# Two blocks on one core: the second projection of the last feed forward by seven products instead of eight, its sums split between VectorE, ScalarE and transfers

## The reference

```python
        h = h + rmsnorm(m, post_mix_g[l])
        f = rmsnorm(h, pre_ff_g[l]) @ w_ff1[l]          # 1024 -> 4096
        f = jnp.square(jax.nn.relu(f)) @ w_ff2[l]       # 4096 -> 1024
        h = h + rmsnorm(f, post_ff_g[l])
```

## Time and profile before

| | us |
|---|---|
| median of 3 runs | 1729.57 (1729.56 to 1731.13) |
| the profiled execution | 1730.73 |
| its span in the profile | 1729.0 |
| TensorE busy | 1715.3 (99%) |
| VectorE busy | 1209.1 (70%) |
| ScalarE busy | 820.2 (47%) |
| GpSimd busy | 46.4 (3%) |
| moved by transfers | 181.36 MB, 105 GB/s in the mean |

### The profile page before, as it was taken

The page is one execution under the profiler, slowest core; times in us unless marked ns, Lnnn a source line. Parts: engine busy times, 40 slices in busy tenths (PEclk is TensorE's granted clock), DMA queues, the critical chain, the costliest instruction groups (busy, mean ns, idle before and its releaser), DMA issues.

```text
span 1729.0 us, 26320 instructions
## 1 busy us (share of the span) xinstructions
PE 1715.3 (99%) x10458; PEld 1497.2 (87%) x10458; DVE 1209.1 (70%) x1975; ACT 820.2 (47%) x1449; POOL 46.4 (3%) x103
## 2 busy tenths in 40 slices
PE   9999999999999999999999999999999999999998
PEld 8777788999999887777989999989888898999997
DVE  4588787777787735666877777868446876677776
ACT  4477744444445235664444444443565555333342
POOL 0212000000000000000000000000000000000000
PEclk9999999999999999999999999999999999999999
DMA  8343332333334232224133333352314224333331
GB/s 276 113 134 118 119 89 87 109 98 110 101 99 153 86 105 84 81 91 122 39 103 98 110 110 97 99 165 82 110 44 140 63 73 126 106 98 98 100 109 49
DMA packets 220125, 181.36 MB, mean 105 GB/s; under 512 B 9906, under 2 KB 178771, under 8 KB 220003
## 3 DMA queue, kind: packets, MB, share of 16 engines
q1 hardware_dynamic: 217954, 175.48, 33.1%
q0 software_dynamic: 2048, 4.20, 0.9%
HBM read 173.32 MB, written 7.38 MB: 105 GB/s over the span
## 4 chain that ended last, share of the span: by engine, by line
PE 93%; DVE 4%; ACT 1%; DMA 1%; issue 1%; POOL 0%; DVEq 0%; POOLq 0%
PE ps L733 29%; PE ps L734 28%; PE ps L735 28%; PE ps L1092 1%; PE ps L1137 1%; PE ps L1163 1%; PE ps L1112 1%; PE ps L1151 1%; DMA arena<-arena 1%; PE ps L987 1%; DVE wlo L1701 0%; DVE xl L1793 0%; PE ps L1102 0%; PE ps L972 0%; ACT whi L1321 0%
## 5 line engine op out<-in xcount | busy, mean ns | idle before, releaser
L1701 DVE TENSOR_TENSOR wlo<-raw,whi 128x1024 fp32r<-128x1024 f32 (+1 forms) x276 | 317.6, 1167 | 181.3 <-ACT whi L1321 181.0
L733 PE MATMUL ps<-xh,whi 128*128 128x256 f32 (+1 forms) x1016 | 332.4, 327 | 2.3 <-DVE xl L1793 2.3
L735 PE MATMUL ps<-xh,wlo 128*128 128x256 f32 (+1 forms) x1016 | 326.1, 321 | 0.0
L734 PE MATMUL ps<-xl,whi 128*128 128x256 f32 (+1 forms) x1016 | 325.9, 321 | 0.0
L1321 ACT ACTIVATE whi<-raw 128x1024 fp32r<-128x1024 f32 (+1 forms) x276 | 274.6, 1007 | 80.9 <-DMA raw<-in_w_ff 36.4
L733 PE MATMUL ps<-whi,hh 128*128 128x512 f32 x728 | 288.7, 397 | 1.4 <-DVE wlo L1701 1.3
L734 PE MATMUL ps<-wlo,hh 128*128 128x512 f32 x728 | 285.2, 392 | 0.0
L735 PE MATMUL ps<-whi,hl 128*128 128x512 f32 x728 | 283.6, 390 | 0.0
L733 PEld LDWEIGHTS ps<-xh,whi 128*128 128x128 f32 x1016 | 194.1, 191 | 25.8 <-issue 8.8
L735 PEld LDWEIGHTS ps<-xh,wlo 128*128 128x128 f32 x1016 | 194.1, 191 | 14.4
L734 PEld LDWEIGHTS ps<-xl,whi 128*128 128x128 f32 x1016 | 194.4, 191 | 12.2
(11 more groups left out here) (272 smaller groups left out, 2935.3 us busy)
## 6 DMA issues: line engine op xcount, KB each, us to landing
raw<-in_ffn_w_in SPq DMA_DIRECT2D x88, 512.0 KB, 3.8
raw<-in_w_ff SPq DMA_DIRECT2D x64, 512.0 KB, 4.2
raw<-in_ffn_w_out SPq DMA_DIRECT2D x44, 512.0 KB, 3.9
raw<-in_a_w_qkv SPq DMA_DIRECT2D x22, 512.0 KB, 5.5
raw<-in_w_in SPq DMA_DIRECT2D x20, 512.0 KB, 3.8
raw<-in_kv_w SPq DMA_DIRECT2D x16, 512.0 KB, 4.1
bias_skewed<-bias_rows SPq DMA_DIRECT2D x8, 640.0 KB
arena<-arena POOLq DMA_DIRECT2D x64, 64.0 KB, 2.7
```

Of the source, the lines that this page charges most:

```text
L733: e.matmul(o, ah, bh, start=start, stop=False, **more)
L734: e.matmul(o, ah, bl, start=False, stop=False, **more)
L735: return e.matmul(o, al, bh, start=False, stop=stop, **more)
L1701: e.tensor_tensor(lo[:, 0:n], src, f32(hi[:, 0:n]), ALU.subtract).then_inc(s.lo, 1)
```

## The change

In groups 1 to 6 the second projection is computed as products of 2 x 2 blocks: tokens 0 to 255 and 256 to 511 by block pairs (b, b+1) and (b+2, b+3) on the left, block pairs by output halves on the right. Seven products take the place of eight (`SEVEN`): a11, a12, s1, s4, s2, s3, a22, each 2 token tiles x 2 blocks x 3 matmuls. Groups 0 and 7 stay as they were.

- **Left sums** (s1, s2, s4, s3): VectorE, `left_sum`, from the unsplit hidden values. Every left operand then gets a high part (ScalarE) and a low part (VectorE) of its own (`left`), issued two products ahead. So the hidden blocks are not split any more when they are made, and `hidden_words` keeps them in float32.
- **Right sums**: B11 + B12, then + B22, then + B21 in one buffer, B12 + B22 in another. SP loads weight tiles into the four parts of `x`, POOL adds the others to them by transfers that add (`accum_op`). Every right operand is split as any weight.
- **Result sums**: two PSUM chains of two banks. After a11, a12 and a22 VectorE adds the bank to the left columns of `mb`. After s1, s4, s2, s3 ScalarE copies the bank with a sign to one of four buffers, and POOL adds this to the right columns of `mb` by a transfer. s4, s2, s3 and a22 go on in the bank that has just been read.
- **Relu and Square** of a pair's blocks move from VectorE to ScalarE (`square_hidden`), where they belong to these groups.
- `x` is written to DRAM ahead of the feed forward and read back at its end (`park`, `unpark`); the last gain vector is loaded late; `FEED_PIECES` becomes "2212", 14 pieces in a turn of two pairs.
- Weights lie in DRAM tile by tile, 4 KB in a row for each partition, so each load is one plain transfer. Some semaphores are shared, and the triangle of the mixer is loaded later.

```diff
-FEED_PIECES = ["1111"] + ["2222"] * 13
+FEED_PIECES = ["1111"] + ["2212"] * 13
+SEVEN_FIRST, SEVEN_LAST = 1, 6
+SEVEN = [("a11", 0, True, 0, 0, 1), ("a12", 1, True, 0, 0, 1), ("s1", 1, True, 1, 1, -1), ("s4", 1, False, 0, 1, -1),
+         ("s2", 0, False, 0, 1, -1), ("s3", 0, False, 1, 1, -1), ("a22", 0, False, 1, 0, 1)]
...
+        rights = [Right(a, ("load", landed), [(a, "a", (first, 1))]), Right(b, ("load", b_need), (), b_next),
+                  Right(a, ("a", 48 * turn + 16), [(a, "a", (last, 1))]),
+                  Right(c, ("load", c_need), [(d, "d", (last, 1))], c_next),
+                  Right(a, ("a", 48 * turn + 32), [(a, "a", (last, 0))]), Right(d, ("d", 16 * turn + 16), (), d_next),
+                  Right(a, ("a", 48 * turn + 48), (), following)]
...
+        for n, (name, chain, start, m, nh, sign) in enumerate(SEVEN):
+            u = 7 * (g - SEVEN_FIRST) + n
+            unit = self.unit("seven", rights[n], None)
...
+            for t in range(2):
...
+                self.step("seven", piece)
...
+                self.step("seven_post", piece)
+                self.flush()
+                if t == 1:
+                    self.left(u + 2)
+                yield
...
+            elif what == "seven":
...
+                w.wait_ge(s.lo, p.unit + 1)
+                w.wait_ge(s.left_lo, p.u + 1)
...
+                for k in (0, 1):
+                    m = mm3(e, ps[b][:], lh[:, k, c], ll[:, k, c], wh[:, k, :], wl[:, k, :], p.start and k == 0, k == 1,
+                            skip_group_check=True)
...
+            elif what == "left":
+                u, name, b, entry, (sem, value), free = arg
+                w.wait_ge(self.events[sem], value)
+                if free:
+                    w.wait_ge(s.rows, free)
+                e.activation(self.left_parts(entry)[0], self.left_source(name, b), ACT.Copy).then_inc(s.left_hi, 1)
...
+                e.activation(self.evict_to(p.sent), ps[p.bank][:], ACT.Copy, scale=float(p.sign)).then_inc(s.evicted, 1)
...
+            elif what == "square_hidden":
...
+                w.wait_ge(s.combined, pair.combined[3])
+                e.activation(first, first, ACT.Relu).then_inc(s.act, 1)
...
+                e.activation(second[:, 256:512], second[:, 256:512], ACT.Relu).then_inc(s.act, 1)
...
+                e.activation(self.hidden_words[:, pair.blocks[0], :], first, ACT.Square).then_inc(s.relu, 1)
...
+                e.activation(self.hidden_words[:, pair.blocks[1], :], second, ACT.Square).then_inc(s.relu, 1)
...
+                if name == "s1":
+                    e.tensor_tensor(tmp, a22, a21, ALU.subtract).then_inc(s.left_sum, 1)
+                elif name == "s2":
+                    e.scalar_tensor_tensor(tmp, tmp, -1.0, a11, ALU.mult, ALU.subtract).then_inc(s.left_sum, 1)
+                elif name == "s4":
+                    e.scalar_tensor_tensor(a12, a12, -1.0, tmp, ALU.mult, ALU.subtract).then_inc(s.left_sum, 1)
+                else:
+                    e.tensor_tensor(a21, a11, a21, ALU.subtract).then_inc(s.left_sum, 1)
...
+                e.tensor_tensor(self.mb[:, p.tile, 0:512], self.mb[:, p.tile, 0:512], ps[p.bank][:],
+                                ALU.add).then_inc(s.fadd, 1)
...
+                e.tensor_tensor(lo, self.left_source(name, b), f32(hi), ALU.subtract).then_inc(s.left_lo, 1)
...
+                    if chain == "a":
+                        w.wait_ge(s.lo, m + 1)
+                    else:
+                        w.wait_ge(s.right[buffer], right.before)
+                    e.dma_start(self.x[:, buffer, :], self.row_tile(*source),
+                                accum_op=ALU.add).then_inc(s.right_sum[chain], 16)
...
+                e.dma_start(self.mb[:, p.tile, p.nh * 512:p.nh * 512 + 512], self.evict_to(p.sent), accum_op=ALU.add).then_inc(s.added[p.sent % 4], 16)
...
+            e.dma_start(self.raw[:, m % RAW, :], ap["c_tiles"][m]).then_inc(s.raw[m % RAW], 16)
...
+            elif what == "park":
+                w.wait_ge(s.add, 8)
+                for t in range(4):
+                    e.dma_start(self.parked[t * 128:t * 128 + 128, :], self.x[:, t, :]).then_inc(s.x, 16)
```

More of the change, by code:

```diff
@@ L61, in __init__ @@
         self.kind, self.nh, self.t, self.bank, self.i = kind, nh, t, bank, i
-        self.norm, self.group, self.value = norm, group, None
+        self.norm, self.group, self.value, self.added = norm, group, None, None
+class Piece:
+    def __init__(self, u, unit, t, bank, start, before, value, tile, nh, sign, sent, earlier, after):
+        self.u, self.unit, self.t, self.bank, self.start, self.before, self.value = u, unit, t, bank, start, before, value
+        self.tile, self.nh, self.sign, self.sent, self.earlier, self.after = tile, nh, sign, sent, earlier, after
+class Right:
+    def __init__(self, buffer, need, sums=(), load=None):
+        self.buffer, self.need, self.sums, self.load, self.before = buffer, need, sums, load, None
 class Pair:
-    def __init__(self, kind, n, table, columns, blocks):
+    def __init__(self, kind, n, table, columns, blocks, first=None):
         self.kind, self.table, self.columns, self.blocks = kind, table, columns, blocks
@@ L350, in rows @@
                 self.step("rows_post", r)
+                if kind == "f" and group == 0:
+                    self.plain_rows = r.value
             yield
@@ L466, in attention_a, with seven, ring @@
         self.run(out)
+    def seven(self, g):
+        def ring(n):
+            k = SEVEN_FIRST + n // 3
+            return None if k > SEVEN_LAST else (n % 2 + 2, (4 * k + (2, 2, 0)[n % 3], (0, 1, 1)[n % 3]))
+        first, last = 4 * g, 4 * g + 2
+        turn, a = g - SEVEN_FIRST, g % 2
+        needs = []
+        for n in range(3):
+            r = 3 * (g - SEVEN_FIRST) + n
+            self.ring_need[r % 2] += 16
+            needs.append((r % 2 + 2, self.ring_need[r % 2], ring(r + 2)))
+        (b, b_need, b_next), (c, c_need, c_next), (d, d_need, d_next) = needs
+        following = (a, (4 * g + 8, 0)) if g + 2 <= SEVEN_LAST else None
+        landed = turn // 2 * 16 + 16
+        rights = [Right(a, ("load", landed), [(a, "a", (first, 1))]), Right(b, ("load", b_need), (), b_next),
[3 more added lines that the diff above has]
+                  Right(a, ("a", 48 * turn + 48), (), following)]
+        rights[3].before = d_need
+        if g == SEVEN_FIRST:
+            self.left(1)
+        for n, (name, chain, start, m, nh, sign) in enumerate(SEVEN):
+            u = 7 * (g - SEVEN_FIRST) + n
+            unit = self.unit("seven", rights[n], None)
+            if g == SEVEN_LAST and n == 6:
+                self.step("gain", self.fifth)
+                self.step("unpark", unit)
+            for t in range(2):
+                if (chain, t) not in self.chains:
+                    self.chains[chain, t] = self.bank(hold=True)
+                bank, tile = self.chains[chain, t], 2 * m + t
+                value, sent = self.count("rows") + 1, self.count("sent") if nh else None
+                after = ("evicted", sent + 1) if nh else ("fadd", self.count("fadd") + 1)
+                piece = Piece(u, unit, t, bank, start, self.evicts.get(bank), value, tile, nh, sign, sent,
+                              self.added.get((tile, nh)), after)
+                self.evicts[bank], self.added[tile, nh] = after, sent if nh else after[1]
+                self.step("seven", piece)
+                if t == 1:
+                    self.done(unit, "rows", value)
+                    self.entry_free[self.entry_of[u]] = value
+                if g == SEVEN_LAST and n == (3 if chain else 6):
+                    self.release(bank)
+                self.step("seven_post", piece)
+                self.flush()
+                if t == 1:
+                    self.left(u + 2)
+                yield
@@ L1314, in scalar @@
                     w.wait_ge(s.raw[tile % RAW], self.raw_at[tile])
+                elif kind == "seven":
+                    what, value = tile.need
+                    w.wait_ge(s.right[tile.buffer] if what == "load" else s.right_sum[what], value)
                 else:
@@ L2259, in sync @@
                 m, = arg
-                _, _, tile = self.plan.units[m]
+                kind, right, tile = self.plan.units[m]
+                if kind == "seven" and right.load is not None:
+                    w.wait_ge(s.hi, m + 1)
+                    w.wait_ge(s.lo, m + 1)
+                    rows_load(*right.load)
                 if tile is not None and tile + RAW < len(self.plan.tiles):
```

379 lines of the change are left out of this document (273 added, 106 removed).

## The result

Changed: 1754.11 us median of 4 runs (1750.48 to 1754.74), before: 1729.72 (1729.56 to 1731.13). The ratio is 1.0135, 95% interval [1.0117, 1.0152]. The change makes the kernel 24 us slower, where 13 were forecast. The profiled execution of the changed kernel took 1750.48 us, its span is 1748.8 with a mean granted clock of 0.996; the other three runs have 0.992 to 0.994, and no trace of them is kept.

What follows compares the result with a forecast made beforehand. TensorE's matmul stream was taken as the bound: 1730.7 - 16.3 (matmuls removed) + 19.0 (turns) + 3.0 (group 6) + 7.5 (clock) = 1743.9, median given as 1743 us. Forecast range 1733 to 1755, overall 1715 to 1763.

Steps and rivals of the forecast that it cites:

- The waits before s1: TensorE in each turn: about 1 us before s1 for a PSUM bank, the rest of 3.8 us before s3.
- the hole: VectorE idle 2.6 us after a pair's last addition, waiting for ScalarE's left high part behind Relu and Square.
- the turn: Two first-projection pairs plus one second-projection group, repeating: 42.08 us before, 39.36 without waits, about 44 to 45 forecast.
- A small wait of some 0.8 that I find before the next a12 is swallowed by the slower matmuls: In the turns, a wait of some 0.8 us before the next a12 was taken to cost nothing beside the slow clock.
- Group 1's first products start behind plain rows with room to spare: 0.: At the entry into the changed groups, no extra waiting of TensorE was expected: 0 us.
- Group 6, 3 us in bounds of 1 to 5: Last changed group: no weight sums for a further pair, but the bank wait and a closely following weight sum remain: +3 us.
- The clock, 7.5 in bounds of 0 to 10: Slower granted clock behind the waits before s3, 1.5 us in each of five turns: +7.5 us.
- If each brings the same: Each gap before s3 was assumed to lose 1.5 us of clock, like the earlier 1.83 us gap before this feed forward.
- granted clock near 0.9 in the stretch: Sign that would show the forecast right: granted clock near 0.9 over the changed stretch of the profile.
- Transfers: Adding 512 KB transfers for second weights: landing in about 5 us, wanted after 5.9, so no cost; 8.4 would hold ScalarE 2.5.
- transfers late: Rival: sums land in 8.4 us or transfer engines are full, 1758 us, with both 1763; range 1755 to 1765, chance 0.20.
- chain hidden, full gain: Rival: hand-overs between engines never hold TensorE, giving 1713 us; chance 0.22 for hidden wholly or in part.

Runs made afterwards that it cites:

- both orders: Changed kernel with the left part two products ahead split before the deferred Relu and Square, and left sums issued half a product earlier: 1730.41 us, ratio 0.9999.
- the square later too: On top of both orders, the deferred Relu and Square also stand behind the split of the next weights: 1726.63 us, ratio 0.9976.
- small transfers: Adding transfers cut to 8 columns, their number and waits kept: on the changed kernel 1748.31 us, on the square later too 1721.44 us.
- later splits: The square later too, two steps moved at group 1's start, group 6's second weights' splits one or two products later: 1720.71 us, ratio 0.9943.

## Why the prediction came out as it did

- **Direction and mechanism: right, by experiment.** TensorE bound, 16.3 us of matmuls out, and a chain of in-order hand-overs that gives back more. Orders alone, with the work the same, took back 24 us (both orders) and 28 (the square later too), 16.3 and 18.6 of them in idle time. The waits before s1 (0.92 with the restart, 1 forecast) and s3 (2.7, 2.8 forecast), the hole (2.57, 2.6 forecast) and the turn (44.8, 44 to 45 forecast) are in the trace.
- **"A small wait of some 0.8 that I find before the next a12 is swallowed by the slower matmuls": the step that failed in the turns.** It stands before a11, costs 0.66 to 1.05, and is swallowed by nothing, since by then the clock is back. 3.9 us. That the turn came out as forecast is therefore in part luck: this wait stands where more of the clock's loss was expected.
- **"Group 1's first products start behind plain rows with room to spare: 0."** Mis-sized: 4.5 us, of which the forecast had about 1 in the turns' 19. VectorE stood 4.7 us for the high part of a12's weight, which ScalarE had behind an eviction and the squares, and then had the sums, splits and additions at once. I had followed a turn in its steady state and not the entry into it.
- **Group 6, 3 us in bounds of 1 to 5:** 4.6, and 5.5 with the bank wait before s1 that the forecast had in this term, so above its upper bound. The reason was only half right: besides the bank and the sum, ScalarE's queue puts evictions behind waits for landings. The runs with small transfers and with later splits give 4 to 5 us for it, clock included.
- **The clock, 7.5 in bounds of 0 to 10:** 4.8 in the profiled run, some 9 in the median. "If each brings the same" was wrong: of five equal gaps the profiled run has two with a slow stretch behind (0.58 and 0.62) and three without; the row of before gave the size of one, not how often. In the changed kernel's profile the very same wait of 1.83 us, at 1377.68, has a clock of 1.00 behind it. The sign "granted clock near 0.9 in the stretch" didn't follow from 7.5 us either, which over the 290 us of the pairs is 0.97; it was 0.99.
- **Transfers:** landing was taken at about 5 us with a decision at 5.9; the median is 5.9, on the edge (6.7 from 1480 to 1680 us). In the turns it costs 0.6 us of the profiled run (two waits before a11), at the end some 5. The four loads into `x` per turn, which I didn't price, take 6.3 us, and the loads into `raw` 5.1 in the same stretch, where a plain load took 4.2. By the Trainium skill, DMA: Bandwidth & Descriptors, Anatomy of one DMA, the estimate for 512 KB was 3.2 us; the trace disagrees, with 5.9 at a transfer share of 0.83. What it gives as fixed, 2.0 us, is near the small sums of 4 KB from DRAM, which landed in 2.3; those within SBUF took 3.2.
- **Sum:** over before, 24.4 us in the median against 13.4. Turns +3.1, group 1 +4.5, group 6 +1.6, clock +1.5 make 10.7 of the 11.0. The forecast's own range (1733 to 1755) holds the result by 0.9 us only, and the range given to the rival "transfers late" begins at 1755; the trace, not the time, tells the two apart. The likeliest value was low because the ends of the stage were not followed as the middle was.
- **The rival "chain hidden, full gain"** falls for this order. (Its "never held TensorE for more than 1.3 us in all" overlooks the 2.3 us of the earlier trace rows; those, too, are waits on VectorE.) As an order it nearly exists: 1720.7 and 1718.8, where 1713 was the full gain.

Not tried: extra buffers for the summed weights in group 6, and the change with only some of the six groups. Why some waits have a slow stretch behind them and others don't stays open.

## What to carry to other kernels

When work moves between two engines that take instructions in order, count hand-overs along the queue, not busy shares: a sum issued half a product ahead of the engine that needs it was worth 19 us, the same sum removed 6 (11 and 4 in TensorE's idle time). Moving one step out of the way moves the hole to the next instruction that waits for the same engine, so follow both queues until an instruction has slack. And price the entry and the exit of a repeated stage by themselves: here they were a quarter of the loss, and the exit had another cause (transfers) than the turns.

## What was new about the hardware

- Equal waits do not bring equal clocks: behind 2.53 us of idle TensorE the granted clock was 0.62 over 4 us, behind 2.54 us it was 1.00, in the same execution. The wait of 1.83 us before this feed forward stands in all 14 profiles of this case: in six of them (before, and five of the experiments) a clock of 0.50 follows for 3.4 us, in the other eight it is 1.00 throughout. So two profiles can differ by up to 1.7 us through such a stretch with the same program up to there.
- A transfer that adds 512 KB from DRAM into SBUF landed in 5.9 us in the median (256 KB of result columns in 6.0) with transfer shares of 0.8 to 0.9, and slowed plain 512 KB loads into `x` beside it from 3.8 (small sums) to 6.3 us. A second one issued some 0.5 us behind another took about 9 in groups 1 to 5.
- GpSimd spends 0.87 us to issue one of them, 10.5 of 42 us in a turn (rows above), and VectorE's operations of 128x1024 kept their 1.22 us beside it.
